# Two value banks, interleaved softmax steps and a later norm sum in a memory-attention block (Trainium2, one core)

## What is computed

```python
def cross_attention(h, mem_n, wq, wk, wv, wo):          # 4 heads of width 256, 256 memory rows
    q = (h @ wq).reshape(bsz, l, XA_HEADS, XA_HEAD_DIM)
    k = (mem_n @ wk).reshape(bsz, m, XA_HEADS, XA_HEAD_DIM)
    v = (mem_n @ wv).reshape(bsz, m, XA_HEADS, XA_HEAD_DIM)
    s = jnp.einsum('blhd,bmhd->bhlm', q, k).astype(jnp.float32) * (XA_HEAD_DIM ** -0.5)
    p = jax.nn.softmax(s, axis=-1).astype(v.dtype)
    o = jnp.einsum('bhlm,bmhd->blhd', p, v).reshape(bsz, l, D_MODEL)
    return o @ wo
...
    x = x + cross_attention(h, mem_n, xa_wq[i], xa_wk[i], xa_wv[i], xa_wo[i])
    h = rmsnorm(x, ffn_norm_w[i])
    x = x + conv_ffn(h, ffn_w_up[i], ffn_conv_w[i], ffn_conv_b[i], ffn_w_down[i])
```

## Time and profile before

| | |
|---|---|
| median of 3 runs | 1645.62 us |
| the profiled execution, its own time | 1644.47 us |
| its span in the trace | 1643.3 us |
| PE busy | 1483.1 us (90%) |
| DVE busy | 1025.0 us (62%) |
| ACT busy | 756.9 us (46%) |
| PE's share of the chain that ended last | 77% |
| mean granted TensorE clock | 0.953 |

### The profile page before, as it was taken

How to read it: one execution, slowest core, us unless ns; L and a number is a source line. 1 busy time by engine, 2 the same in 40 slices (tenths; PEclk the granted TensorE clock), 3 DMA queues, 4 the chain that set the end, 5 groups by cost and what they waited for, 6 DMA issues and landing times.

```text
span 1643.3 us, 17536 instructions
## 1 busy us (share of the span) xinstructions
PE 1483.1 (90%) x6907; PEld 1159.9 (71%) x6907; DVE 1025.0 (62%) x1354; ACT 756.9 (46%) x994; POOL 121.9 (7%) x143
## 2 busy tenths in 40 slices
PE   6999879989888999999999998999988699999981
PEld 4776558768666788788878787885547578888861
DVE  4888774654324565446545658836444688988876
ACT  5453344644323322112214543244445578888763
POOL 1500000000000000000000303200000011111012
PEclk8999989899999999999999999999999799999996
DMA  5222122202102342232223221210003599999984
GB/s 209 77 77 77 51 101 79 102 27 93 61 26 77 115 142 79 88 128 97 76 71 104 78 103 54 75 52 27 26 1 143 212 362 418 411 409 412 408 306 179
DMA packets 39329, 231.57 MB, mean 141 GB/s; under 512 B 4400, under 2 KB 5696, under 8 KB 17104
## 3 DMA queue, kind: packets, MB, share of 16 engines
q1 hardware_dynamic: 30640, 200.09, 32.5%
q0 software_dynamic: 7648, 27.87, 4.6%
q10 hardware_dynamic: 960, 2.49, 0.4%
HBM read 213.66 MB, written 16.78 MB: 140 GB/s over the span
## 4 chain that ended last, share of the span: by engine, by line
PE 77%; DVE 12%; ACT 5%; issue 3%; DMA 2%; POOL 0%; POOLq 0%; ACTq 0%; DVEq 0%
PE bank L416 15%; PE bank L417 14%; PE bank L418 14%; PE bank L2915 5%; PE bank L2917 5%; PE bank L2916 5%; PE bank L562 3%; DVE w_lo L372 2%; PE bank L435 1%; PE bank L2166 1%; PE bank L2195 1%; PE bank L436 1%; PE bank L437 1%; PE bank L815 1%; PE bank L802 1%
## 5 line engine op out<-in xcount | busy, mean ns | idle before, releaser
L416 PE MATMUL bank<-h_hi,w_hi 128*128 128x512 f32 x952 | 389.2, 409 | 29.4 <-DVE h_lo L496 13.6
L417 PE MATMUL bank<-h_lo,w_hi 128*128 128x512 f32 x952 | 378.9, 398 | 0.0
L418 PE MATMUL bank<-h_hi,w_lo 128*128 128x512 f32 x952 | 378.9, 398 | 0.0
L372 DVE TENSOR_TENSOR w_lo<-w_raw,w_hi 128x2048 fp32r<-128x2048 f32 (+3 forms) x89 | 196.3, 2206 | 92.6 <-ACT w_hi L366 92.0
L416 PEld LDWEIGHTS bank<-h_hi,w_hi 128*128 128x128 f32 x952 | 181.9, 191 | 83.1 <-issue 15.9
L418 PEld LDWEIGHTS bank<-h_hi,w_lo 128*128 128x128 f32 x952 | 181.6, 191 | 42.8
L417 PEld LDWEIGHTS bank<-h_lo,w_hi 128*128 128x128 f32 x952 | 182.1, 191 | 41.3 <-issue 1.9
L366 ACT ACTIVATE w_hi<-w_raw 128x2048 fp32r<-128x2048 f32 (+3 forms) x89 | 158.3, 1779 | 60.0 <-PE bank L418 60.0
L3095 DVE TENSOR_TENSOR h_lo<-w_raw,h_hi 128x2048 fp32r<-128x2048 f32 x32 | 73.3, 2292 | 15.3 <-ACT h_hi L2996 15.3
L3095 DVE TENSOR_TENSOR lo_b<-raw_b,hi_b 128x2048 fp32r<-128x2048 f32 x32 | 73.2, 2288 | 8.6 <-ACT hi_b L2996 8.6
L416 PE MATMUL bank<-a_hi,w_hi 128*128 128x512 f32 x176 | 69.6, 395 | 4.5 <-DVE a_lo L1607 4.5
(11 more groups left out here) (579 smaller groups left out, 2809.4 us busy)
## 6 DMA issues: line engine op xcount, KB each, us to landing
w_raw<-in_params_dram SPq DMA_DIRECT2D x122, 1024.0 KB, 4.9
raw_b<-in_params_dram SPq DMA_DIRECT2D x51, 1024.0 KB, 8.0
w_raw<-in_params_dram SPq DMA_DIRECT2D x16, 704.0 KB, 4.0
result_rows<-osb POOLq DMA_DIRECT2D x16, 512.0 KB, 8.2
result_rows<-prm POOLq DMA_DIRECT2D x8, 512.0 KB, 3.1
xt<-in_x_t_dram POOLq DMA_DIRECT2D x1, 2048.0 KB, 10.0
scratch_rows<-htm SPq DMA_DIRECT2D x4, 512.0 KB, 3.0
out_dram<-pr SPq DMA_DIRECT2D x4, 512.0 KB, 2.6
```

Of the source, the lines that this page charges most:

```text
L372: V.tensor_tensor(k.w_lo[:, g % SPLIT, 0:size], k.raw[:, g % RAW, 0:size], k.w_hi[:, g % SPLIT, 0:size].bitcast(F32), ALU.subtract).then_i ...
L416: PE.matmul(ps, wh, hi[:, c, 0:width], start=c == 0, stop=False)
L417: PE.matmul(ps, wh, lo[:, c, 0:width], start=False, stop=False)
L418: m = PE.matmul(ps, wl, hi[:, c, 0:width], start=False, stop=c == parts - 1)
```

## The change

The second half of a head's values goes to bank 6 instead of bank 7, so that it no longer waits for the first half; instead the first transposes of the next head, which write bank 6, wait for both halves' `lo`. Steps 12 to 15 of the attention stand behind 4-chunk parts of the first four `wo` blocks, and steps 16 and 17 each ahead of two 2-chunk parts. The split of slot 1 of `wo` stands behind step 12, and each later split stands one block earlier, ahead of the residual of an odd block. The norm sum stands behind the first column of `up0`.

```diff
+def out_bank(k, n):
+    return k.bank[7 - n % 2][:, :]
...
+            if h and t == 0:
+                PE.wait_ge(s.o_lo, OUT["at"] + 2 * h)
             for j in range(2):
                 m = pe_turn(k, k.bank[6][:, j * P:j * P + P], k.pa[:, i % 3, j * P:j * P + P])
...
-                    PE.wait_ge(s.at_sc if n == 0 else s.o_lo, 1 if n == 0 else OUT["at"] + n)
-                    PE.matmul(k.bank[7][:, :], k.vtm[:, 0, n * P:n * P + P], k.pt[:, h % 2, 0, :], start=True, stop=False)
...
+                    if n == 0:
+                        PE.wait_ge(s.at_sc, 1)
+                    PE.matmul(out_bank(k, n), k.vtm[:, 0, n * P:n * P + P], k.pt[:, h % 2, 0, :], start=True, stop=False)
...
 # pe_memory
-    next(steps)
-    next(steps)
     for b in range(4):
-        pe_fm(k, "wo", b // 2, b % 2, k.hi, k.lo, stop=6, after="at" if b == 0 else None)
+        pe_fm(k, "wo", b // 2, b % 2, k.hi, k.lo, stop=4, after="at" if b == 0 else None)
         next(steps)
+    for b0 in (0, 2):
+        next(steps)
+        for b in (b0, b0 + 1):
+            pe_fm(k, "wo", b // 2, b % 2, k.hi, k.lo, first=4, stop=6, after="at" if b == 0 else None)
     for b in range(DB):
         pe_fm(k, "wo", b // 2, b % 2, k.hi, k.lo, first=6 if b < 4 else 0, after="at" if b == 0 else None)
-    pe_norm_sum(k, "ffn", k.sq, T, 7)
...
 # act_memory (dve_memory alike)
+    next(steps)
     act_split_to(k, SLOT0["wo"] + 1)
     for _ in steps:
         pass
     for b in range(DB):
-        act_split_to(k, SLOT0["wo"] + b // 2 + 1)
+        act_split_to(k, SLOT0["wo"] + (b + 1) // 2 + 1)
         act_residual(k, "wo", b, "ffn", k.col("ffn_norm", 0, DB))
...
 # pe_ffn
                 pe_fm(k, up, j, part, k.hi2, k.lo2, "ffn" if half == 0 and j == 0 else None, at=part * DB * P, cols=P)
+            if half + j == 0:
+                pe_norm_sum(k, "ffn", k.sq, T, 7)
```

More of the change, by code:

```diff
@@ L1348, with score_bank @@
 AT_SCALE = (D // XA_H) ** -0.5
+def score_bank(k, i):
+    return k.bank[4 + i % 2][:, 0:MEM]
+def out_bank(k, n):
+    return k.bank[7 - n % 2][:, :]
 def pe_attention(k):
@@ L1359, in pe_attention @@
                 PE.wait_ge(s.sm_exp, i - 1)
-            ps = k.bank[4 + i % 2][:, 0:MEM]
+            ps = score_bank(k, i)
             PE.matmul(ps, k.qt[:, 2 * h, t * P:t * P + P], k.kt[:, 2 * h, :], start=True, stop=False)
@@ L1375, in pe_attention @@
                     n = 2 * h + d
-                    PE.wait_ge(s.at_sc if n == 0 else s.o_lo, 1 if n == 0 else OUT["at"] + n)
-                    PE.matmul(k.bank[7][:, :], k.vtm[:, 0, n * P:n * P + P], k.pt[:, h % 2, 0, :], start=True, stop=False)
-                    PE.matmul(k.bank[7][:, :], k.vtm[:, 1, n * P:n * P + P], k.pt[:, h % 2, 1, :], start=False, stop=True).then_inc(s.at_o, 1)
+                    if n == 0:
+                        PE.wait_ge(s.at_sc, 1)
+                    PE.matmul(out_bank(k, n), k.vtm[:, 0, n * P:n * P + P], k.pt[:, h % 2, 0, :], start=True, stop=False)
+                    PE.matmul(out_bank(k, n), k.vtm[:, 1, n * P:n * P + P], k.pt[:, h % 2, 1, :], start=False, stop=True).then_inc(s.at_o, 1)
         yield
@@ L1390, in act_attention @@
                 A.wait_ge(s.sm_t, i - 2)
-            A.activation(k.pa[:, i % 3, :], k.bank[4 + i % 2][:, 0:MEM], ACT.Exp, bias=k.st[:, 0, i % 3:i % 3 + 1], scale=k.asc[:, 1, t:t + 1],
+            A.activation(k.pa[:, i % 3, :], score_bank(k, i), ACT.Exp, bias=k.st[:, 0, i % 3:i % 3 + 1], scale=k.asc[:, 1, t:t + 1],
                          accum_out=k.st[:, 1, i % 3:i % 3 + 1]).then_inc(s.sm_exp, 1)
@@ L1404, in act_attention @@
                     A.wait_ge(s.at_o, n + 1)
-                    A.activation(k.hi[:, n, :], k.bank[7][:, :], ACT.Copy).then_inc(s.o_hi, 1)
+                    A.activation(k.hi[:, n, :], out_bank(k, n), ACT.Copy).then_inc(s.o_hi, 1)
         yield
@@ L1418, in dve_attention @@
                 V.wait_ge(s.sm_exp, i - 2)
-            v(V.tensor_reduce(mx, k.bank[4 + i % 2][:, 0:MEM], AX.X, ALU.max))
+            v(V.tensor_reduce(mx, score_bank(k, i), AX.X, ALU.max))
             v.own()
@@ L1433, in dve_attention @@
                     V.wait_ge(s.o_hi, OUT["at"] + n + 1)
-                    V.tensor_tensor(k.lo[:, n, :], k.bank[7][:, :], k.hi[:, n, :].bitcast(F32), ALU.subtract).then_inc(s.o_lo, 1)
+                    V.tensor_tensor(k.lo[:, n, :], out_bank(k, n), k.hi[:, n, :].bitcast(F32), ALU.subtract).then_inc(s.o_lo, 1)
         yield
@@ L1514, in dve_memory @@
     for b in range(DB):
-        dve_split_to(k, SLOT0["wo"] + b // 2 + 1)
+        dve_split_to(k, SLOT0["wo"] + (b + 1) // 2 + 1)
         dve_residual(k, "wo", b, "ffn", k.col("ffn_norm", 0, DB))
```

## The result

| | before | changed |
|---|---|---|
| median of the runs beside each other | 1645.86 us (4 runs) | 1630.73 us (4 runs, 1629.19 to 1631.76) |
| ratio, with its 95% interval | | 0.9913 (0.99 to 0.9927) |
| the profiled execution's span | 1643.3 us | 1630.6 us |
| mean granted TensorE clock | 0.953 | 0.951 |

The change makes the kernel 15.1 us faster by the medians, 12.7 us in the two profiled executions. The prediction was 1629.6 us, 16.0 us less than before.

What follows compares the result with a forecast made beforehand. PE was taken as the bound (77% of the chain that ended last), with time won at its stalls and low clock. Terms 7.8 + 4.4 + 0.7 - 1.0 + 1.4 + 2.7 = 16.0 us less: median 1629.6 us, range 1625 to 1635.

Steps and rivals of the forecast that it cites:

- A: Values of each head: with two banks the second half no longer waits for the first; 7.8 us less over four heads.
- B: Attention steps 12 and 13: the 4.73 us stall moves to step 13 and is 1.9 us; 4.4 us less.
- E: Split of slot 2 of wo: starts earlier, leaving a 2.1 us stall at block 4; 1.4 us less.
- a half keeps PE for 1.43 us: Values of a head: without the wait the second half would start at 426.36, 1.96 us less per head.
- I count the 0.4 us as won as well: First value matmul behind the step 13 stall: 1.13 us instead of 1.52, as 1.9 us should leave the clock alone.
- C: End of step 17: 12 wo matmuls cover the 0.72 us wait for the last lo; 0.7 us less.
- D: Step 16, following step 15 with nothing between: its transposes wait for DVE's scaling; 1.0 us more, bounds 0 and 1.7.
- F: Norm sum behind up0's first column: 4.05 us less there, 1.35 us lost to the late root; 2.7 us less.
- the first (falls at the shorter stalls): Rival, chance 0.13: clock also falls at step 13 and in the first up0 block, 1.6 to 1.7 us each; 1632.9 us.
- The second (late root): Rival, chance 0.10: Ln's table loads only behind the norm sum, up0's slot 2 comes 2.7 us later; 1632.3 us.
- The third (better): Rival, chance 0.04: the fall at block 4 of wo goes too, step 16 waits 0.5 us less; 1627.5 us.
- The fourth (the clock low through the stretch): Rival, chance 0.02: short waits from 460 us on hold the clock low, 25 us more; 1654.6 us.

Runs made afterwards that it cites:

- four edits: The changed kernel with last split behind the last residual, norm sum one block earlier, ACT's split of slot 1 first, wo part before step 16: 1623.88 us, ratio 0.9869.

## Why the prediction was right

The time lies 1.1 us over the forecast, in the range, and the mechanism of each term was found where it was placed. That the total is so near is partly luck: A and B together brought 2.6 us less than forecast, and E 1.6 us more, by a fall of the clock that did not come. By terms, measured in the trace after and by the experiments:

- **A, two banks: 6.7 us, forecast 7.8.** The step that failed is "a half keeps PE for 1.43 us". That took the next block's start, 0.46 us behind the last value matmul (428.11 to 428.57 after), as the pace of value matmuls. Between value matmuls the starts lie 0.86 us apart (426.39, 427.25, 428.11); the first matmul behind them starts early in the record, but takes 0.79 us, and its cost shows there. A half behind the first costs 1.72 us and not 1.43.
- **B, steps 12 and 13: about 2.9 us, forecast 4.4.** The stall's place and length held (1.96 for 1.9 us), and the values of head 2 start 3.9 us sooner: 469.58 - 460.74 = 8.84 us behind step 12's turn before, and 468.36 - 457.79 = 10.57 us now, 5.6 of which are the 24 matmuls that came from later (their first starts 0.14 us behind the transposes at 457.65). "I count the 0.4 us as won as well" failed. The clock fell behind that stall too; the first value matmul (468.36 to 470.23) was 0.5 us slower than in the kernel before, itself slow there, and the second (to 471.60) 0.5 us slower than in the other heads.
- **C, 0.7 us, and D, -1.0 us:** held. No wait at the end of step 17, and 0.96 us at step 16; its removal showed it as a cost of its own. Both values here are idle times of the rows; from start to start C is 0.9 us and D 1.2, which leaves the sum as it is.
- **E, block 4 of wo: 3 us in the profiled execution, forecast 1.4.** The stall is 2.11 for 3.46 us. The fall of the clock, which I left in, did not come there, 1.6 us more. In the execution with four edits it came behind the same 2.11 us. B and E are the same open question, with its two answers: a fall at the 1.96 us stall, none at 2.11.
- **F, norm sum: 2.8 us, forecast 2.7.** From the start of up0 to its third column 28.86 us before (17.66 and a column of 11.2), 547.95 - 521.92 = 26.03 now. Within it the waits for `h_lo` cost 1.78 us from start to start, 1.8 forecast, the last wait 0.81 (0.64 in its row) for 1.35, and the sum costs PE some 0.4 us more than the 0.45 taken, for the same reason as in A: 535.54 to the next L416 at the usual pace is 0.70 us, in fact it took 1.10. The forecast's 13.15 us for the column is 0.15 more than its own terms (11.2 + 1.6 + 0.2); the column took 13.16 (521.92 to 535.08), so the slip came out right by chance.

The sum is 6.7 + 2.9 + 0.7 - 1.0 + 3.0 + 2.8 = 15.1 us, for a stretch that is 15.13 us shorter.

Of the rivals, the first (falls at the shorter stalls) held in half: at step 13, not in the first up0 block. The second (late root) did not: 0.64 us, and Ln starts 1.06 us behind the sum's start, with its table loaded before. The argument against it was weaker than it looked: the 1.33 us of before held a load (537.80 to 539.08) that ran beside the sum. The third (better) held in half too: the fall at block 4 did not come, but step 16 waited its full 0.96 us. The Trainium skill's price of a table switch (ScalarE: Activation LUTs, "What ACT_TABLE_LOAD costs"), 2.66 us with a drain, again differs from the rows: Ln ends at 536.83, Exp starts at 538.14, 1.31 us. The fourth (the clock low through the stretch) did not come: the granted clock over the stretch is 0.99, more than the 0.98 before. The mechanism that the Trainium skill describes (TensorE: Matmul & The Clock Gate, "A second HAM failure mode: psum-queue depth-cycling"), a clock that oscillates from short pauses between groups, is not seen in this stretch: its falls stand behind waits of 1.96 us and more (the one at step 13 with a wait of 0.47 us close behind it).

Not settled is what decides whether a wait of about 2 us brings a fall. The fall behind the 1.96 us at step 13 came in all eight profiled executions that kept this wait; behind the 2.11 us at block 4 it came in one of ten. The granted clock was 1.00 and 0.76 behind the same 2.11 us, and 1.00 and 0.65 behind the same 2.24 us, where it fell in seven of fourteen. The rows show one difference: behind the 1.96 us come transposes of 0.44 us and then another wait of 0.47 us, and the 2.11 us have no such wait behind them. The 0.47 us alone is not the cause, since it stands there also where the stall is filled and the clock holds. Whether the two together are was not tested.

## What to carry to other kernels

A stall that is moved is worth its new length, and that can be worked out ahead from the chain that ends it: here five waits came out within 0.75 us, four of them within 0.2 of the lengths forecast for their rows. When a split or another preparation is moved ahead of work in an in-order queue, look for the place at which it waits for the very block whose result the work behind it needs; the last one of the series cost 1.5 to 2 us here, while the first gained. After such a change read the new stalls of 1 to 2 us, put independent work ahead of them in parts as long as the stall, and compare the stretch that was touched rather than the whole run, in which falls of the clock elsewhere are worth as much.

## What the runs showed of the hardware that was not expected

The clock falls differently in stretches that the change does not touch: over the part behind the stretch, the profiled executions took 977.42 us before and 979.35 us changed, with the same instructions, and the same wait of 2.24 us (2.23 in one) was followed by a fall in 7 of 14 executions, at a cost of about 1.7 us. The fall behind the 1.96 us at step 13 cost between 1.4 and 3.1 us. And a value matmul (x2 in its row, 0.86 us from start to start) is followed in the record by a matmul that starts after 0.46 us and takes 0.79: in such rows the start of the next kind of matmul does not give the pace of the one before.
